# Two units in step in the first and last feed-forward block, and a re-ordered second memory attention

## What is computed

```python
# first layer
x = x + 0.5 * swiglu(rms(x) , ffn1)            # f=0, ni=0: the first block of the kernel
x = x + (gated sum of sparse attention, conv, memory attention) @ w_out
x = x + 0.5 * swiglu(rms(x), ffn2)             # f=1, ni=2
# second layer
x = x + mixer(rms(x))                          # windowed attention and gated recurrence, @ w_mix_o
q = rms(x) @ w_mem_q                           # 4 heads of 64
k, v = split(rms(mem) @ w_mem_kv)              # 256 memory rows
x = x + (softmax(q k^T / 8) v) @ w_mem_o       # the second memory attention
x = x + (silu(rms(x) @ w_gate) * (rms(x) @ w_up)) @ w_down   # f=2, ni=5: the last block
return rms(x)
```

## Time and profile before

| | |
|---|---|
| median of three executions | 2561.86 us |
| profiled execution, its own time | 2556.7 us |
| its span, first to last instruction | 2554.9 us |
| PE busy | 2460.6 us, 96% |
| DVE busy | 1412.0 us, 55% |
| ACT busy | 962.9 us, 38% |
| POOL busy | 173.1 us, 7% |
| mean granted TensorE clock | 0.982 |

### The profile page before, as it was taken

The page is one execution under the profiler, slowest core; times in us unless marked ns, Lnnn a source line. Parts: engine busy times, 40 slices in busy tenths (PEclk is TensorE's granted clock), DMA queues, the critical chain, the costliest instruction groups (busy, mean ns, idle before and its releaser), DMA issues.

```text
span 2554.9 us, 31373 instructions
## 1 busy us (share of the span) xinstructions
PE 2460.6 (96%) x12046; PEld 2055.1 (80%) x12046; DVE 1412.0 (55%) x2965; ACT 962.9 (38%) x1784; POOL 173.1 (7%) x236
## 2 busy tenths in 40 slices
PE   7999999999999999989999999999998997999997
PEld 6888888888887878778888888878876886788886
DVE  5435555676567566765443446666543566543444
ACT  4323334432344444553322334655422345322321
POOL 0000000100001111220000000222100002000000
PEclk9999999999999999999999999999998999899998
DMA  3454433333321111103223224211121341223222
GB/s 131 119 123 128 111 110 137 102 105 112 103 75 62 50 58 67 46 28 113 99 88 102 99 88 138 68 51 58 56 77 66 116 140 50 79 88 106 99 85 89
DMA packets 86093, 231.36 MB, mean 91 GB/s; under 512 B 8456, under 2 KB 23432, under 8 KB 85946
## 3 DMA queue, kind: packets, MB, share of 16 engines
q1 hardware_dynamic: 78480, 217.18, 26.1%
q10 hardware_dynamic: 7466, 12.19, 2.4%
HBM read 217.79 MB, written 11.53 MB: 90 GB/s over the span
## 4 chain that ended last, share of the span: by engine, by line
PE 87%; DVE 7%; ACT 3%; issue 2%; POOL 1%; ACTq 0%; DMA 0%; SPq 0%; DVEq 0%
PE bank L912 86%; PE bank L1082 1%; DVE t_pp L1943 1%; DVE t_PS L1739 1%; POOL t_pw L2327 1%; ACT t_pp L1492 1%; DVE t_wlo L1734 1%; ACT t_PS L1372 0%; ACT t_whi L1372 0%; DVE t_tmp L1783 0%; DVE t_QS L2036 0%; DMA t_raw<-in_f_in 0%; ACT t_XH L1372 0%; PE bank L1253 0%; ACT t_tmp L1372 0%
## 5 line engine op out<-in xcount | busy, mean ns | idle before, releaser
L912 PE MATMUL bank<-t_XH,t_whi 128*128 128x512 f32 x2064 | 819.0, 397 | 22.9 <-DVE t_XL L1743 19.6
L912 PE MATMUL bank<-t_XL,t_whi 128*128 128x512 f32 x2064 | 808.8, 392 | 0.0
L912 PE MATMUL bank<-t_XH,t_wlo 128*128 128x512 f32 x2064 | 808.6, 392 | 0.0
L1734 DVE TENSOR_TENSOR t_wlo<-t_raw,t_whi 128x1024 fp32r<-128x1024 f32 (+2 forms) x420 | 481.7, 1148 | 417.0 <-ACT t_whi L1372 413.9
L1372 ACT ACTIVATE t_whi<-t_raw 128x1024 fp32r<-128x1024 f32 (+2 forms) x420 | 415.5, 991 | 453.3 <-PE bank L912 406.5
L912 PEld LDWEIGHTS bank<-t_XH,t_whi 128*128 128x128 f32 x2064 | 391.0, 189 | 107.7 <-issue 15.0
L912 PEld LDWEIGHTS bank<-t_XH,t_wlo 128*128 128x128 f32 x2064 | 390.7, 189 | 83.5
L912 PEld LDWEIGHTS bank<-t_XL,t_whi 128*128 128x128 f32 x2064 | 391.2, 190 | 78.1
L912 PE MATMUL bank<-t_RX,t_whi 128*128 128x512 f32 x1056 | 325.0, 389 | 0.0
L1813 DVE TENSOR_TENSOR t_tmp<-bank,t_RB 128x512 f32<-128x512 f32 x178 | 122.5, 688 | 233.6 <-PE bank L912 231.3
L912 PEld LDWEIGHTS bank<-t_RX,t_whi 128*128 128x128 f32 x1056 | 198.2, 188 | 41.2
(11 more groups left out here) (305 smaller groups left out, 2752.4 us busy)
## 6 DMA issues: line engine op xcount, KB each, us to landing
t_raw<-in_f_in SPq DMA_DIRECT2D x88, 512.0 KB, 3.2
t_raw<-in_f_out SPq DMA_DIRECT2D x32, 384.0 KB, 3.1
t_raw<-in_w_conv SPq DMA_DIRECT2D x24, 512.0 KB, 3.2
t_raw<-in_w_merge SPq DMA_DIRECT2D x24, 512.0 KB, 3.2
t_raw<-in_fg SPq DMA_DIRECT2D x22, 512.0 KB, 3.2
t_raw<-in_fu SPq DMA_DIRECT2D x22, 512.0 KB, 3.2
t_raw<-in_f_out SPq DMA_DIRECT2D x32, 320.0 KB, 2.8
t_raw<-in_w_g SPq DMA_DIRECT2D x16, 512.0 KB, 3.2
```

The costliest lines, as they stand in the source:

```text
L912: return e.matmul(o, l, r, start=start, stop=stop, skip_group_check=True)
L1734: e.tensor_tensor(wlo[n % NRAW][:, 0:width], raw[n % NRAW][:, 0:width], f32(whi[n % NHI][:, 0:width]), ALU.subtract).then_inc(*w_lo.tick(n))
```

## The change

- Feed-forward blocks with ni in EACH (0 and 5) start with a step `pair`: for each k, the three matmuls of the first a unit and the three of the first b unit, into banks 6 and 7. The squares and sums become a step of their own, `normsq`, and stand behind the pair for these two norms; `nstat` comes after the next a unit, `nspread` after the next b unit, and the first `ffg` after that. For the other norms normsq follows norm directly, as before.
- A step `start` sets the beginning by hand on all engines: the first two units are loaded, copied and subtracted in halves of 512 columns, mixed with the rows of x; TensorE runs WARM = 6 matmuls of zeros. vec is issued by ScalarE's queue first, cst by SyncE's behind the rows, relx and onehot after the first ffg (`relload`).
- The second memory attention: mv2(0) runs between nstat and nspread of norm 4; mv2(1), mv2s and mq2s(1) run inside the attention, ahead of tiles 2 and 3. Scores of heads 0 and 1 wait for the first half of q and k only. mmo is cut in two halves by k: the first halves of m = 0, 1, 2 run within the attention, those of 3 to 7 behind it. norm(5, m-1) follows mmo(m). `w.both` lets a step with two units count as if the second were not there yet, so that splits don't run too far ahead.

```diff
+EACH = (0, 5)
+WARM = 6
     def add_units(self, kind, args, ns):
-        self.items.append(((kind, *args, *ns), len(self.units)))
+        self.items.append(((kind, *args, *ns), len(self.units) - self.both))
     def ffn(f, ni, wa, wb, wo, oa, ob, nxt, jobs):
+        late = []
                 first = h == 0 and m == 0
+                if first and ni in EACH:
+                    n, n2 = w.unit(wa, oa), w.unit(wb, ob)
+                    w.both = 1
+                    w.add_units("pair", (f,), [n, n2])
+                    for k in range(KD):
+                        w.add("normsq", ni, k)
+                    w.both = 0
+                    late = [one("ffg", f, h, 0)]
+                    continue
                 w.lin("ffa", f, h, m, name=wa, j=oa + h * KF + m)
+                if late:
+                    w.add("nstat", ni)
...
-                if first:
+                if first or late:
+                    w.add("nspread", ni)
+                while late:
+                    late.pop()()
+                    if f == 0:
+                        w.add("relload")
     def mem2_keys():
...
-        for j in range(2):
-            w.lin("mv2", j, name="w_mv2", j=j)
-        w.add("mv2s")
-        yield
     def memory2(nxt):
+        w.lin("mq2", 0, name="w_mq2", j=0)
+        w.add("nstat", 4)
+        w.lin("mv2", 0, name="w_mv2", j=0)
+        w.add("nspread", 4)
+        w.add("mq2s", 0)
+        w.lin("mq2", 1, name="w_mq2", j=1)
+        def first_out():
+            w.add("om", 0)
+            n.append(w.unit("w_mmo", 0))
+            w.later += [lambda: None] * 2 + [one("mmo", m, n[0], 0) for m in range(3)]
+        at = [{2: lambda: w.lin("mv2", 1, name="w_mv2", j=1), 3: both(one("mv2s"), one("mq2s", 1))}, {}, {}, {}]
+        after = [{}, dict(after=first_out), {}, dict(after=one("om", 1))]
+        attend([Head("mm2", h, range(4), h=h, at=at[h], **after[h]) for h in range(4)], [])
+        w.catch_up()
+        n.append(w.unit("w_mmo", 1))
+        w.both = 1
+        for m in range(3, 6):
+            w.add("mmo", m, n[m // 4], 0)
         for m in range(KD):
+            if m > 4:
+                w.both = 0
+            if m > 5:
+                w.add("mmo", m, n[1], 0)
+            w.add("mmo", m, n[m // 4], 1)
+            if m:
+                norm(nxt, m - 1)
+        norm(nxt, KD - 1)
# TensorE
+        def start():
+            b = take("d", ("start",))
+            for _ in range(WARM):
+                mm(b[:, 0:256], ZER[:, 0:P], ZER, True, True)
+        def pair(f, n, n2):
+            a, b = take("s", ("ffa", f, 0, 0)), take("s", ("ffb", f, 0, 0))
+            for k in range(KD):
+                c = slice(k * P, (k + 1) * P)
+                operand(("n", (0, 2, 5)[f], k))
+                for o, unit in ((a, n), (b, n2)):
+                    hi, lo = weights(unit) if f or k > 3 else first_half(unit)
+                    done = three(o, hi[:, c], lo[:, c], XH[:, k, :], XL[:, k, :], k == 0, k == KD - 1)
# scores of the second memory attention
-                operand(("mq2", 1))
-                operand(("mk2", 1))
+                operand(("mq2", h // 2))
+                operand(("mk2", h // 2))
# ScalarE (VectorE the same with the low parts)
+        def start():
+            half(0, 0)
+            norm(0, 0)
+            half(1, 0)
+            norm(0, 1)
+            norm(0, 2)
+            half(0, 1)
+            norm(0, 3)
+            half(1, 1)
+            for k in range(4, KD):
+                norm(0, k)
# SyncE
+        half(0, 0)
+        rows(0)
+        half(1, 0)
+        rows(1)
+        rows(2)
+        half(0, 1)
+        rows(3)
+        half(1, 1)
+        for k in range(4, KD):
+            rows(k)
+        e.dma_start(cst, A["cst"]).then_inc(*d_c.tick(0, by=16))
```

More of the change, by code:

```diff
@@ L280, in ffn, with norm @@
                 if h:
-                    w.add("norm", nxt, m)
+                    norm(nxt, m)
+    def norm(ni, k):
+        w.add("norm", ni, k)
+        if ni not in EACH:
+            w.add("normsq", ni, k)
     def mem_norm(i):
@@ L1345, in mq2, with mmo @@
             dense(("mq2", q), n, *X, ("n", 4))
-        def mmo(m, n):
+        def mmo(m, n, k):
             hi, lo = weights(n)
-            b = take("d", ("mmo", m))
-            operand(("om", 0))
-            operand(("om", 1))
-            for k in range(2):
-                c = slice((2 * (m % 4) + k) * P, (2 * (m % 4) + k + 1) * P)
-                f = three(b, hi[:, c], lo[:, c], OM[0][:, k, :], OM[1][:, k, :], k == 0, k == 1)
-            f.then_inc(*full.tick(("mmo", m), *([("u", n)] if m % 4 == 3 else [])))
-        do = dict(banks=set_banks, nstat=nstat, nspread=nspread, memstat=memstat, ffa=ffa, ffb=ffb, ffo=ffo, conv=conv,
+            b = banks[("mmo", m)] if k else take("d", ("mmo", m), True)
+            operand(("om", k))
+            c = slice((2 * (m % 4) + k) * P, (2 * (m % 4) + k + 1) * P)
+            f = three(b, hi[:, c], lo[:, c], OM[0][:, k, :], OM[1][:, k, :], k == 0, k == 1)
+            if k:
+                f.then_inc(*full.tick(("mmo", m), *([("u", n)] if m % 4 == 3 else [])))
+                banks.let_go(("mmo", m))
+        do = dict(banks=set_banks, nstat=nstat, nspread=nspread, memstat=memstat, start=start, pair=pair, ffa=ffa, ffb=ffb, ffo=ffo, conv=conv,
                   convg=convg, wide=wide, widestat=widestat, widefin=widefin, memv=memv, mgate=mgate, score=score,
@@ L1775, in rsqrt, with half, start @@
             newton(R, *s[0:4], dst, result, r1)
+        def half(n, h):
+            c = slice(512 * h, 512 * h + 512)
+            done = n if h else (n, 0)
+            on.wait_ge(*w_hi.at(done))
+            e.tensor_tensor(wlo[n][:, c], raw[n][:, c], f32(whi[n][:, c]), ALU.subtract).then_inc(*w_lo.tick(done))
+        def start():
+            half(0, 0)
+            norm(0, 0)
+            half(1, 0)
+            norm(0, 1)
+            norm(0, 2)
+            half(0, 1)
+            norm(0, 3)
+            half(1, 1)
+            for k in range(4, KD):
+                norm(0, k)
+            e.tensor_scalar(gqn[:, 0:1], v("gq"), -0.125, None, ALU.mult).then_inc(*calc.tick(("gqn", 0)))
+            e.tensor_scalar(gqn[:, 2:4], v("gmq", 0, 2), -1.0 / 16, None, ALU.mult).then_inc(*calc.tick(("gqn", 1)))
+            e.tensor_scalar(gqn[:, 4:6], v("ggla", 0, 2), 0.5, None, ALU.mult).then_inc(*calc.tick(("gqn", 2)))
+            e.tensor_scalar(negs, v("sink", 0, 16), -1.0, None, ALU.mult).then_inc(*calc.tick(("negs",)))
+            e.tensor_scalar(bg2, v("bg2", 0, 16), 0.5, None, ALU.mult).then_inc(*calc.tick(("bg2",)))
         def norm(ni, k):
@@ L2377, in final, with rows, half @@
             e.dma_start(out[k * P:(k + 1) * P, :], XT[:, k, :]).then_inc(*d_o[k].tick(0, by=16))
-        e.dma_start(vec, A["vec"]).then_inc(*d_vec.tick(0, by=16))
-        n = 0
-        for k in range(KD):
+        def rows(k):
             e.dma_start(XT[:, k, :], A["xT"][k * P:(k + 1) * P, :]).then_inc(*d_x[k].tick(0, by=16))
-            if k % 2 == 0 and n < NRAW:
-                load(n)
-                n += 1
+        def half(n, h):
+            name, j, _, _ = unit[n]
+            c = slice(512 * h, 512 * h + 512)
+            e.dma_start(raw[n][:, c], A[name][j, :, c]).then_inc(*d_half[2 * n + h].tick(0, by=16))
+        half(0, 0)
+        rows(0)
+        half(1, 0)
+        rows(1)
+        rows(2)
+        half(0, 1)
+        rows(3)
+        half(1, 1)
+        for k in range(4, KD):
+            rows(k)
+        e.dma_start(cst, A["cst"]).then_inc(*d_c.tick(0, by=16))
+        n = 2
         do = dict(table=table, msplit=msplit, final=final)
```

74 lines of the change are left out of this document (36 added, 38 removed).

## The result

The changed kernel takes 2535.9 us (median, 2535.3 to 2537.0) against 2561.5 for the kernel before in the same turns: ratio 0.990, 95% interval 0.9883 to 0.9917. The profiled execution took 2536.2, its span is 2534.4.

What follows compares the result with a forecast made beforehand. TensorE, 96% busy, was taken as the bound, so only its idle moments and low-clock stretches could move the time. Gains 9.2 + 1.5 + 7.8 = 18.5 us gave 2538.2 profiled, 2543.4 for usual runs; range 2536 to 2554.

Steps and rivals of the forecast that it cites:

- A: Kernel start, to the first RX matmul: first two units paired and loaded in halves, gain 9.2 us.
- M: Untouched middle, first RX matmul to first OG matmul: the change touches nothing there, no gain forecast.
- B: End of second mixer, first OG to last OA matmul: projection 3.2 us earlier without mv2, 1.7 clock loss charged, gain 1.5.
- C and D: Second memory attention and last feed-forward block, last OA to last RX matmul: gain 9.8 us, 7.8 after a clock charge.
- E: Rest of the kernel after the last RX matmul: no gain forecast.
- The rival of a start paced by loads: Start: halves land with full units, first matmul at 10 or later, gain 3 there, total 2549 to 2556 us; chance 0.07.
- rival (1): Start, second mixer's end, attention and last block: clock costs more, gain only 11.8, some 2550 us; chance 0.20.
- Part C: Re-ordered second memory attention: 4.9 us later (GpSimd ends 39.5, first second-half 45.3), but six projection triples already done.
- Part D: Last feed-forward pair: operands every 1.36 us instead of 2.74, pair ends at 64.4 after the first mq2 matmul.
- I charge 2.0, between 0 and 5: Attention and last block: TensorE nearly empty from 19.0 to 25.5, so low clock expected, 2.0 us taken off the 9.8.
- The same step gives 2543.4: Whole kernel: 5.2 us, shown runs' median 2561.9 above the profiled time, added to 2538.2.
- Rival (2): Whole kernel: no clock loss at all, gain 22.2 us and up to 1 from loads, 2539 us; chance 0.15.

Runs made afterwards that it cites:

- the three with both holes: Changed kernel with mv2(0) ahead of the second mixer's projection and mv2(1) before norm 4's spread, in three variants of later steps: 2532.6, 2532.0, 2531.9 us.

## Why the prediction was off

By the ruler, with the mean of the two traces of before and of all traces that have the same program in the stage:

| | forecast | measured |
|---|---|---|
| A | 9.2 | 9.8 (139.9 to 130.1) |
| M | 0 | -0.3 (1829.2 to 1829.5) |
| B | 1.5 | 1.9 (144.75 to 142.85) |
| C and D | 7.8 | 11.0 (425.2 to 414.2) |
| E | 0 | 0.0 |
| sum | 18.5 | 22.4 |

- **Part A held**, step by step: start 6.28 for 6.65, pair's end 17.90 for 18.5. The step "the first half unit, vec and row 0 are there at about 5.1" was too late by 0.4 us (ScalarE starts XH at 4.67), and that is most of the 0.6. I had assumed the clock high when the products begin; it rose only at about 7.2, behind the second product. That cost nothing that can be seen, since in the trace of the projection not halved it rose at 4.5 and A is 130.0 as well. Without the dummies it would have been 1.8 of the 2 us that I named as the risk. The rival of a start paced by loads (first matmul at 10 or later) falls.
- **Part B held in its size.** Counted from the first OG the projection started 4.0 earlier (97.6 for 101.6) rather than 3.2, since ScalarE copies the first pieces before the last XT is there; a low stretch of 3.4 us came as charged. In the four traces of that program in which B is 143.3 to 143.6 it was 6.8 us, the second stretch of rival (1). Whether the longer hole is its reason stays open: with the old hole of 1.9 us it is absent in two traces and there, 3.4 us long, in four (mv2 in the mixer and the three with both holes).
- **Part C held**: 39.7 for 39.5, 45.5 for 45.3. What I had not seen is what this means: the move of mv2 gains in B what it costs in C (back in the mixer it is 0.3 us longer in sum), and the halved projection brings 0.8 of the 4.1 us that the sum seemed to give it.
- **Part D held at 2.4 GHz** (64.0 for 64.4). The step that failed is the last one, "I charge 2.0, between 0 and 5". The low stretch came at 2126.9, but it ended under GpSimd's pace, and the granted clock was 1.00 from 2133.7 on. Measured from the same trace of the kernel before as the forecast, C and D gain 9.9 (424.1 to 414.2), where the forecast without any loss was 9.8: the charge was 0. The two traces of that program with 3.4 us less of low clock in CD bear this out, since their CD is not shorter (414.3 and 414.5). The other 1.1 of the 11.0 in the table come from averaging two traces of the kernel before, of which the second is 2.2 longer, 1.5 of it in the attention and 0.7 in the last block.
- **The base.** "The same step gives 2543.4" carried over the 5.2 us by which the three executions shown lie above the profiled one. That is a property of these executions: over the 56 of the kernel before in all turns the median is 2559.2, 2.6 below 2561.9, and only five are at or below the profiled 2556.7. 2559.2 less 22.4 is 2536.8; the changed kernel's nine executions have the median 2536.2.

So of the 7.5 us between forecast and result, 3.2 are the term C and D (2.0 the charge, 1.1 the second trace of the kernel before), 0.7 are A, M, B and E together, 2.6 are the base, and 1.0 is left within the spread of executions. Rival (2), no clock loss, was the nearest, with 2539 by its sum; it left out the base too, and it had no loss in B, where there was one. The low end of the range, 2536, doesn't follow from it either: 22.2 and 1 off 2561.9 are 2538.7. One reading was off as well, though nothing hangs on it: the longest low stretch of the kernel before is not 13.6 us, the last one runs for 14.3 to the end of its trace, with TensorE nearly idle.

The rule of the Trainium skill that I weighed (TensorE: Matmul & The Clock Gate, section Why this matters for your kernels: no idle gaps between bursts) fits these traces only in part. The low stretches do stand behind the new holes, of 3.68 and 2.37 us. But the one in C costs nothing, because GpSimd paces the tiles then, and the one in B also comes behind a hole of 1.9 us. And the kernel before pays in shorter gaps of its own: behind those of the earlier trace rows its second unit starts its triples 1.28 apart instead of 0.68 for a while. That loss is inside the 75.8 us that the forecast subtracted from, so it was not forgotten; what was left out is that it differs between executions.

What stays open: which part of CD's 2.2 us between the two traces of before is usual. The 2.6 us by which the median of its executions lies above the profiled one would fit, but only two executions have a trace.

## What to carry to other kernels

Cut both traces at the same few instructions and compare stages before explaining a difference in spans; a stage that the change doesn't touch shows how large chance is. When TensorE's clock is charged to a new idle gap, ask which engine sets the pace behind it: where another one does, the low clock costs nothing. Don't take the base from three executions when single ones differ by 10 us. An early start that is paid with work on the engine without slack (VectorE among the tiles) was worth nothing here: fill a hole only with steps whose follow-up work, copies and reciprocals included, fits a hole too.

## What the runs showed of the hardware

The granted clock also falls where TensorE shows no idle time. Busy time by stretch of the kernel after, in the untouched middle: 14.5 us fully busy at 1.00, then 6.8 us fully busy at 0.50.

```profile
740.00:754.50 14.50, 14.50 (x96) 12.90 (x94) 8.82 (x28) 8.77 (x23) 3.87 (x6) 1.00 0.22 74
754.73:761.55 6.82, 6.82 (x21) 5.74 (x22) 4.41 (x27) 1.91 (x5) 1.02 (x2) 0.50 0.00 1
```

(A matmul's end is modelled in the trace, so "busy" here says only that no gap shows.) Such stretches stand near the same places in every trace, but their number and length differ from one execution of the same instructions to the next: in M they sum to 61.4 us in the trace where M is shortest (1825.2) and to 81.9 where it is longest (1834.7). M ranges over 9.5 us, 0.4% of this kernel, and it is the largest part of what the traces with one program differ by.

The record of the granted clock begins with its first rise, and the view shows 1.00 before that. At the start of a kernel the clock has to be read from the distances of the matmuls, 0.43 or 0.23 us here.

A low clock costs time only where TensorE sets the pace: 3.4 us more of it in B made B 1.0 to 1.4 longer, 3.4 us more in CD, beside GpSimd's tiles, made CD no longer.
